# A mixture-of-experts trunk: the first expert's start, with one weight remainder on GpSimd, two loads behind a gather, and fewer unread products

## The reference

```
scores = sigmoid(t @ w_router)                      # t: (384, 1024), 16 experts in 4 groups
... pick one group, then the top 2 experts inside it; gate = normalised scores of the two
hg = t @ w_gate[e];  hu = t @ w_up[e]               # for each expert e, 1024 x 512 each
a  = silu(hg) * hu * gate[:, e]
y  = sum over e of a @ w_down[e]                    # 512 x 1024
```

## Time and profile before

| | |
|---|---|
| median of 3 runs | 1150.08 us (1149.22 to 1152.48) |
| time of the profiled execution | 1151.39 us |
| its span, first to last instruction | 1149.4 us |
| mean granted TensorE clock | 0.977 |
| TensorE matmuls busy | 1076.3 us, 94% of the span |
| VectorE busy | 851.3 us, 74% |
| ScalarE busy | 689.6 us, 60% |
| GpSimd busy | 153.1 us, 13% |

### The profile page before, as it was taken

The page is one execution under the profiler, slowest core; times in us unless marked ns, Lnnn a source line. Parts: engine busy times, 40 slices in busy tenths (PEclk is TensorE's granted clock), DMA queues, the critical chain, the costliest instruction groups (busy, mean ns, idle before and its releaser), DMA issues.

```text
span 1149.4 us, 16080 instructions
## 1 busy us (share of the span) xinstructions
PE 1076.3 (94%) x5979; PEld 846.3 (74%) x5981; DVE 851.3 (74%) x1191; ACT 689.6 (60%) x866; POOL 153.1 (13%) x184
## 2 busy tenths in 40 slices
PE   6999989897999999999989998799799999999996
PEld 4798454683788888888869975477378888888885
DVE  5345656667799888888965456766778988889896
ACT  2333555544577778777724365654357777777764
POOL 0326100320011111111040011000001111111002
PEclk8999999998999999999989999999899999999998
DMA  9997889258589999999698381005768999999951
GB/s 348 341 341 218 326 289 296 56 188 347 212 334 371 365 375 368 380 379 381 229 364 244 129 253 58 1 1 196 312 236 314 371 382 369 376 379 371 372 203 57
DMA packets 82560, 319.86 MB, mean 278 GB/s; under 512 B 22464, under 2 KB 26926, under 8 KB 69692
## 3 DMA queue, kind: packets, MB, share of 16 engines
q1 hardware_dynamic: 67232, 285.58, 67.8%
q0 software_dynamic: 14160, 30.19, 7.7%
q10 hardware_dynamic: 1100, 3.23, 0.7%
HBM read 308.05 MB, written 30.57 MB: 295 GB/s over the span
## 4 chain that ended last, share of the span: by engine, by line
PE 79%; issue 7%; DVE 6%; ACT 4%; DMA 3%; SPq 1%; POOL 0%; DVEq 0%; ACTq 0%; POOLq 0%
PE bank L1211 16%; PE bank L1203 15%; PE bank L1204 15%; PE bank L921 3%; PE bank L917 3%; PE bank L914 3%; PE bank L1259 3%; PE bank L1094 2%; PE bank L891 2%; PE bank L1108 2%; ACT work L1601 2%; DMA ring<-in_w_in 2%; PE bank L986 2%; PE bank L1126 2%; PE bank L1027 1%
## 5 line engine op out<-in xcount | busy, mean ns | idle before, releaser
L1661 ACT ACTIVATE work_r<-ring 128x4096 fp32r<-128x4096 f32 x94 | 341.6, 3634 | 126.9 <-PE bank L1204 100.1
L2236 DVE TENSOR_TENSOR ring_r<-ring,work_r 128x4096 fp32r<-128x4096 f32 x92 | 403.9, 4416 | 0.0
L1203 PE MATMUL bank<-work_r 128*128 128x512 f32 x768 | 306.2, 399 | 3.2 <-issue 2.9
L1204 PE MATMUL bank<-work_r 128*128 128x512 f32 x768 | 301.1, 392 | 0.0
L1211 PE MATMUL bank<-ring_r,work_r 128*128 128x512 f32 x768 | 195.2, 396 | 4.2 <-DVE ring_r L2236 4.2
L1211 PEld LDWEIGHTS bank<-ring_r,work_r 128*128 128x128 f32 x768 | 144.2, 189 | 37.4 <-DVE ring_r L2236 5.0
L1203 PEld LDWEIGHTS bank<-work_r 128*128 128x128 f32 x768 | 145.3, 189 | 33.9 <-issue 2.9
L1204 PEld LDWEIGHTS bank<-work_r 128*128 128x128 f32 x768 | 145.0, 189 | 29.0
L2498 POOL DMA_INDIRECT work<-hscr,idx x32 | 36.0, 1125 | 377.4 <-PE bank L1259 266.1
L1517 ACT ACTIVATE work_r<-ring 128x512 fp32r<-128x512 f32 (+1 forms) x48 | 28.8, 603 | 71.8 <-PE bank L921 71.7
L1935 DVE TENSOR_TENSOR ring_r<-ring,work_r 128x512 fp32r<-128x512 f32 (+1 forms) x48 | 32.1, 676 | 50.7 <-ACT work_r L1517 50.6
(11 more groups left out here) (268 smaller groups left out, 1538.9 us busy)
## 6 DMA issues: line engine op xcount, KB each, us to landing
ring<-in_w_gate SPq DMA_DIRECT2D x32, 2048.0 KB, 10.1
ring<-in_w_up SPq DMA_DIRECT2D x32, 2048.0 KB, 10.6
ring<-in_w_down SPq DMA_DIRECT2D x32, 2048.0 KB, 10.6
ring<-in_w_ada SPq DMA_DIRECT2D x24, 2048.0 KB, 10.0
ring<-in_w_in SPq DMA_DIRECT2D x4, 2048.0 KB, 15.1
yscr<-hT POOLq DMA_DIRECT2D x2, 3072.0 KB, 13.0
ring<-yscr SPq DMA_DIRECT2D x6, 1024.0 KB, 7.2
ring<-in_w_out SPq DMA_DIRECT2D x4, 1280.0 KB, 6.9
```

What stands on the lines that cost most here:

```text
L1203: mm(b[:], x_hi[:, k, :], hi[:, k, half, :], start=(k == 0), stop=False)
L1204: last = mm(b[:], x_lo[:, k, :], hi[:, k, half, :], start=False, stop=False)
L1661: A_(w_hi[:, slot % 2, :], ring[slot][:], ACT.Copy).then_inc(s_hi, 1)
L2236: tt(ring_r[slot][:], ring[slot][:], w_hi[:, slot % 2, :].bitcast(F32), ALU.subtract).then_inc(s_lo, 1)
```

## The change

Six edits. SP's load of expert 0's down weights, and so all loads behind it, waits until the gather of expert 0's rows has landed. The unread products ahead of expert 0 go from 24 to 10. In layer 0, VectorE adds up the modulation pieces of route[3] after `first_expert_low(1)` and no longer before `onehots(1)`; layer 1 keeps its order. GpSimd makes the remainder of expert 0's up chunk, in the first pass, after the gather of expert 1, once the upper part is there and the gate chunk's remainder has been counted. VectorE no longer makes it, and waits for GpSimd's count before `rest(1, 0)`.

```
                             if p == 0 and isinstance(i, int) and (e, kind) == (1, 2):
-                                sp.wait_ge(s_hscr, 16 * NT * (l + 1))
+                                sp.wait_ge(gathers(l, 0)[0][0], gathers(l, 0)[1][0] + 16)
...
-                        for _ in range(24):
+                        for _ in range(10):
                             mm(bG[:], onesb[:], swab[:], start=True, stop=True)
...
                     onehots(0)
                     slots(0)
                     if p == 0:
-                        for j in route[2] if l else route[3]:
+                        for j in route[2] if l else []:
                             ada(l, j)
...
                         first_expert_low(1).then_inc(s_lo, 1)
+                        for j in route[3]:
+                            ada(l, j)
...
                     tokens_rest(0)
-                    rest(0, 1, 1)
+                    if p:
+                        rest(0, 1, 1)
                     onehots(3)
...
                     slots(2)
+                    if p == 0:
+                        v.wait_ge(s_lo, chunk_no(l, 0, 0, 1) + 1)
                     rest(1, 0, place(0, 0)[0])
...
+                        if (p, e) == (0, -1):
+                            m = chunk_no(l, 0, 0, 1)
+                            g.wait_ge(s_hi, m + 1)
+                            g.wait_ge(s_lo, m)
+                            nc.gpsimd.tensor_tensor(ring_r[1][:], ring[1][:], w_hi[:, 1, :].bitcast(F32), ALU.subtract).then_inc(s_lo, 1)
```

## The result

The changed kernel takes 1144.55 us (median of 14 runs, 1142.1 to 1147.21), where the kernel before took 1152.62 us in 14 runs (1147.9 to 1157.35). The ratio is 0.9934 with a 95% interval of 0.992 to 0.9948: 7.6 us faster, between 6 and 9.2. The forecast was -6.8 us. The kernel before has a median 2.5 us higher in these 14 runs than in the first three of them alone, which are the 1150.08 us that the forecast started from. So the measured time is to be read against 1152.62 us, by the ratio.

The account below looks back on a forecast made before the run. TensorE, busy 279.9 of 282 us in a stretch of experts, was the bound, so only its start could move: -2.3 - 4.6 + 0.1 = -6.8 us, 1150.08 to 1143.3. The range went from -8.5 us to a time of 1149.5.

Parts of the forecast that it names:

- The loads wait for the gather: SP's loads held back: layer 1's gather takes 4.2 us instead of 9.4, and the later loads cost 0.
- Layer 1: Start of expert 0's first product in layer 1: 4.7 us earlier, taken as 4.6.
- Layer 0: Start of expert 0's first product in layer 0: 2.3 us earlier, at 288.6.
- the risk of the clock: Rival: TensorE may lack 2.4 GHz before layer 1's first product, giving -3 instead of -4.6, 1144.9 us; chance 0.12.
- S: Start of expert 0's first product in a layer: 290.92 in layer 0 and 834.70 in layer 1 before the change.
- The modulation pieces: Layer 0, VectorE: with the two pieces moved later, TensorE is let go at 283.9 instead of 283.25, costing 0.65 us.
- GpSimd's subtraction: 8.9 us on GpSimd, holding VectorE's operations with two SBUF inputs; TensorE waits 0 in layer 0, 0 to 0.2 in layer 1.
- The gather that isn't quicker: Rival: the 9.4 us are the gather's own latency, so layer 1 gains nothing: -2.3, 1147.8 us; chance 0.09.
- GpSimd blocking the count: Rival: in layer 1 GpSimd holds VectorE's one-element cast of the count until 837.3: 1153.3 to 1154.3 us; chance 0.10.
- GpSimd being much slower: Rival: the subtraction takes longer than its rows say; at 10.8 us -4.2, 1145.9 us; chance 0.08 for 10 us or more.
- The ring: Rival: the held-back loads come too late for TensorE, costing what is missing of 11 us; answered no, no chance given.

Follow-up runs that it names:

- u4_pieces_early: The changed kernel with layer 0's modulation pieces back at their old place ahead of the onehots on VectorE: ratio 0.9948, 1147.6 us.
- o3_only_load_wait: The kernel before with only SP's loads made to wait for the gather: ratio 0.9969, 1146.94 us.
- three profiles with the same order: The changed kernel with GpSimd's part undone (0.9937), with loads not waiting for the gather (0.9985), and with rest(1, 1) ahead of turned_rest(0) and GpSimd's part undone (0.9862).
- the later cast: The changed kernel with the reduction ahead of VectorE's cast of the count done five times instead of once: ratio 0.9939, 1146.02 us.
- the profile with three: The changed kernel with rest(1, 1) ahead of turned_rest(0), GpSimd's part undone and 3 unread products in layer 0 instead of 10: ratio 0.9859, 1136.46 us.

## Why the prediction was right, point by point

The forecast was -6.8 us and the ratio gives -7.6, with 6 to 9.2 as its interval. By the profiles the two starts give 5.0 us in layer 1, and 0.7 to 2.4 in layer 0 by the clock of the execution, so 5.7 to 7.4. The mechanism is the forecast one; that the sum came within 1 us is in part luck.

- **The loads wait for the gather.** This was right, and the largest term. The forecast was 4.2 us for the gather, it took 4.43. The later loads cost nothing: in the list of waits neither TensorE nor ScalarE waits for an expert's weights. One reading was off: the 5.3 us of layer 0 was not with one load in flight throughout, as the kernel before issued gate 2 at 280.76, 2.3 us into that gather. With none in flight the same gather takes 3.3 to 3.5 us (`u4_pieces_early`, `o3_only_load_wait`, the changed kernel). Undone, the edit costs 0.9985 / 0.9934, 5.9 us by the two ratios.
- **Layer 1.** Forecast 4.6, measured 12.0 - 7.0 = 5.0 us in the profile. Two small errors nearly cancel in it: TensorE turned the rows 4.5 us after the issue and not 4.2, and the 0.5 us for turnings at 1.2 GHz didn't come, as they took 1.16 us, as before.
- **Layer 0.** Forecast 2.3. At full clock the distance was 10.1 us in three profiles with the same order, 2.4 less than before; in the changed kernel's own profile it was only 0.7 less, because the ten unread products ran at half speed (3.93 us for 2.15). The mechanism was right, and the size holds for an execution whose clock is up there. The forecast had put the risk of the clock into layer 1 alone, and priced it there with a slip: S at 831.1 plus 1 us is 2.6 us gained, not 3.
- **The modulation pieces.** The step was costed at 0.65 us lost. Its worth is the 2.2 us that VectorE would be late without it, and 1.6 more for the clock that falls in that wait; the sum held the first and did not name it, and had not seen the second.
- **GpSimd's subtraction.** Forecast 8.9 us, measured 8.94 and 9.01. That it stops VectorE's operations with two inputs in SBUF was right, 3.8 us in layer 0 and 7.1 in layer 1, and so was what is left for TensorE: 0 and 0.26 us, where 0 and 0 to 0.2 were forecast.
- **The rivals.** The gather that isn't quicker fell with 4.43 us. GpSimd blocking the count fell with the later cast, which took 0.15 us inside the subtraction. GpSimd being much slower fell with 9.01 us. The clock is real, and came in layer 0. The ring didn't run dry.

What I did not see is that ten products alone make the kernel slower. The argument looked at when the products end, not at how long TensorE then idles if the rows, or VectorE, aren't there, nor at the clock that this costs.

## What to carry to other kernels

When a small transfer and large loads share the DMA engines and the small one is awaited, hold the large ones back if the rows show them needed much later: here 2 loads, needed more than 10 us after they landed, had doubled a gather's time. A wait of TensorE can cost more than its length, if the clock falls behind it: the 2.7 us of `u4_pieces_early` cost 1.6 more. Products that only fill a wait should last about as long as the wait; change the wait first and the filler after it. Where the wait is gone, as in layer 0, few are needed: the profile with three has the shortest distance, 8.7 us, though its time can't be told from that with ten. Work moved to GpSimd isn't taken off VectorE if VectorE's next operations read two inputs from SBUF; a cheaper cure was to swap two operations of VectorE's own.

## What the runs showed of the hardware

A VectorE cast of one element and one subtraction with an operand in PSUM kept their times (0.15 us, and 1.29 us for two) while GpSimd subtracted 128 x 4096, and the comparisons with both inputs in SBUF stood still until it had ended. The Trainium skill, "SBUF — State Buffer", section "Who interferes with whom", names casts among the operations that can enter a mode with both ports and then contend, when their operands meet its conditions; whether a cast of one element does, the section leaves open, and this one was not held (0.15 us, begun 0.8 us into the subtraction). TensorE, after 6.3 us without work, took 1.97 us for eight turnings and 2.37 for six unread products, where 1.16 and 1.46 are usual. After 2.65 and 2.73 us without work it began the first product of expert 0 at full clock, and then the clock fell to half while it was busy.

A gather of one expert's rows landed 3.3 to 4.5 us after its issue with no load in flight, and 9.4 to 10.2 us after it with two loads of 2048 KB issued just ahead.
